# A two-block network on one core: x loaded first, stage ends by token block, two norm sums on GpSimd

## The chip, the core and the metric

The kernel runs on one NeuronCore of a Trainium2 chip, in Bass, with every engine programmed by hand and every dependence written as a semaphore. Below, PE is TensorE (its matmuls), PEld its weight loads, DVE is VectorE, ACT is ScalarE, POOL is GpSimd and SP is SyncE, which issues most DMAs. The metric is the device time of one execution in microseconds (us); less is better.

## The reference, cut to what matters

256 tokens of width 1024 pass through two blocks; all is float32.

```
x   = x + rms_norm(mix(rms_norm(x) @ w_in) @ w_out)          # NSA, pooling and SGU mixers
x   = x + rms_norm(memory_attention(rms_norm(x), mem) @ w_mo) # stage "mo"
x   = x + rms_norm((gelu(conv(h @ w_up)_gate) * conv(h @ w_up)_val) @ w_down),  h = rms_norm(x)  # "up", "down"
h   = concat(16 meta tokens, x)                               # 272 tokens from here
h   = h + (silu(z) * b * conv(c * xin)) @ conv_out_w          # proj = rms_norm(h) @ conv_in_w
h   = h + mlstm(rms_norm(h) @ mlstm_in_w) @ mlstm_out_w       # 4 heads, 8 gate columns
out = rms_norm(h)[16:]
```

`rms_norm(x) = x * rsqrt(mean(x^2) + eps) * gain`. The kernel leaves the factor 1/rms out of an operand and multiplies it into the product, so the sum of squares of a norm is needed only after the first products that use the new x.

## The kernel before, in words

**Weights.** 287 chunks of 128x1024 float32 go through four slots. SP loads chunk n into `raw` (after `lo_ready` of chunk n-4), ACT copies it to `w_hi` (rounded to fp32r, `hi`, after `chunk_done` of chunk n-4), DVE writes the rest, `w_lo = raw - w_hi` (`lo`). PE forms each product in three fp32r matmuls: hi with hi, hi with lo, lo with hi. ACT and DVE run three chunks ahead of PE (`ahead`). Chunks have an order by name in `_LAYOUT`: kc, vc, vsw, ... mo, up, down, conv_in, conv_out, lk, lq, ...

**Opening.** SP issues the gains (first 80 columns of params), chunk 0, both halves of x (k tiles 0 to 3 and 4 to 7), then chunks 1 to 3. ACT makes `XH` (hi of gain times x) for eight k tiles, DVE makes `XL`. PE first runs `keep_warm(WARM_START)`, products of constants that nothing reads, then chunk kc, one k tile at a time, as `normed_lo` grows; then vc and vsw.

**Stage ends of mo and down** (`rows_stage`, u = 0 and 1). These two stages put tokens on the partitions. The output has two column halves and two blocks b of 128 tokens. In the second half each chunk is used for block 0 and then for block 1. ACT squares the finished block (`rows_norm`, L736), takes the root (L739), DVE inverts it and scales (`rows_update`, L1965 to L1969), ACT scales one part of block 1 (L743), PE turns the blocks back (L1297), DVE adds them to the residual XR (L1974), ACT makes XH (L700) and DVE XL (L1910). PE then runs `side_by_side`: the first three chunks of the next stage together, k tile by k tile, as XH (`raw_hi`) and XL (`raw_lo`) come.

**Norm sums.** ACT writes squares of x into `SQ` and counts `sq_ready`. In `stat_x` PE sums all eight k tiles with 64 recorded small matmuls against ones (32 products); in `stat_sum` GpSimd has added k tiles 0 to 6 into `SS` before (`sum_squares`, six additions, each waiting for the last), and PE needs 8 products. Before the change, norms X2 (after mo) and H0 (after down) use `stat_x`, and H1 (after conv_out) uses `stat_sum`. ACT takes the root, DVE inverts it, PE spreads it (`spread_rstd`, L1214), ACT copies it into `rstd`.

**GpSimd's order** around this: sums of the first norm; during up, 44 elementwise operations (L615, L617); then the DMA of the mLSTM gate weights (`lgate_w`), their scaling (L628), four memsets and the mask built by affine selects (L634, L637); then one multiplication in each round of conv_in (L642).

**H1 and the mLSTM gates.** After conv_out PE runs chunk lk 0 whole, then `gate_products` (L1354) and `stat_sum`; the spread stands in the middle of lk 1. DVE can empty the accumulator of lk 0 (L2431) only when `rstd` is there; there are two accumulators, so lk 2 waits for it.

Of the kernel before, what the change touches and what calls it, by code (L numbers as in the profile page):

```python
# [87 lines left out]
WARM_START = 10  # L88
# [50 lines left out]
def build(nc, weights, x_in, mem_in, meta_in, params, final_gain, rel_bias, onehot, lgate_w, out, bias_rows):  # L139
    with ExitStack() as ctx:  # L140
# [193 lines left out]
        def spread_mem():  # L334
# [9 lines left out]
        gate_loaded, gate_scaled, gate_summed, l_gate_summed, gate_parted = (  # L344
            sem("gate_loaded"), sem("gate_scaled"), sem("gate_summed"), sem("l_gate_summed"), sem("gate_parted"))
# [158 lines left out]
        def _(sp):  # L504
# [42 lines left out]
        def _(pool):  # L547
# [63 lines left out]

            def ffn_pool(p, i, hidden, rest):
# [12 lines left out]
            pool.dma_start(lgate_raw, lgate_w).then_inc(gate_loaded, 16)  # L625
            pool.wait_ge(gate_loaded, 16)
# [30 lines left out]
        def _(act):  # L657
# [403 lines left out]
            for m in range(KT):  # L1061
                ahead(CHUNK["lq"] + m)
                if m == 0:
                    act.wait_ge(l_gate_summed, 1)
# [134 lines left out]
        def _(pe):  # L1199
# [68 lines left out]
            def rows_stage(name, u, per, x, ready):  # L1268

                t = TILE[name]  # L1270
                for half in range(2):
                    o = [acc(t + b)[:, :] if half == 0 else SC[:, span(b, 512)] for b in range(2)]
                    for c in range(per):
# [4 lines left out]
                        for b in range(2):  # L1278
# [4 lines left out]
                            if half and b == 0 and c == per - 1:  # L1283
                                last.then_inc(rows_half, 1)
                        last.then_inc(chunk_done, 1)
                keep_warm(WARM, PTB)
                for b in range(2):
                    for k in range(KT):
# [9 lines left out]
                        if b and k % 2:  # L1298
                            last.then_inc(rows_turned, 1)
                keep_warm(WARM_SPREAD)  # L1300
# [48 lines left out]
            def gate_products(raw_w):  # L1349
# [6 lines left out]
                last.then_inc(gate_summed, 1)  # L1356
# [75 lines left out]
            chunk(CHUNK["kc"], TILE["kc"], xh, xl, S, ready=x_ready)  # L1432
# [284 lines left out]
            stat_x(NORM_H0, 3, T)  # L1717
# [8 lines left out]

            for m in range(KT):
                chunk(CHUNK["lk"] + m, TILE["lk"] + m, xha, xla, T, between=(lambda: spread_rstd(NORM_H1, T)) if m == 1 else None,
                      ready=raw_ready(RAW_H1) if m == 0 else None)
                if m == 0:  # L1730
# [1041 lines left out]
```

## Time and profile before

| | |
|---|---|
| median of 3 runs | 923.64 us (923.40 to 923.68) |
| profiled execution, its own time | 922.43 us |
| its span | 920.70 us |
| PE busy | 908.9 us, 99% |
| DVE busy | 655.7 us, 71% |
| ACT busy | 532.2 us, 58% |
| POOL busy | 131.6 us, 14% |
| mean of DMA traffic | 171 GB/s |

How to read it: the span runs from the first to the last recorded instruction; the profiled execution took 1.73 us more than its span and 1.21 us less than the median. A matmul's record is longer than the distance to the next one, since matmuls are pipelined, so PE's busy share hides short gaps: distances between starts tell more.

### The profile page before, as it was taken

The page shows a single profiled execution, that of the slowest core. Times are in us where ns is not written, and L with a number is a line of the kernel's source. Part 1 is how long each engine was busy: PE and PEld are TensorE (multiplying, and loading weights), DVE is VectorE, ACT ScalarE, POOL GpSimd, SP SyncE. Part 2 cuts the span into 40 slices and gives each one's busy share as a digit, 9 for nine tenths or more (in the row PEclk, how much of TensorE's full clock was granted, in tenths as well). Part 3 has the DMA queues.
Part 4 walks back from the last instruction along what each step waited for, and adds up shares of the span by engine and source line. Part 5 has one row for each costly group of instructions (what it writes and reads, how often), then busy time and mean ns, then how long its engine had stood idle before and what let it go on. Part 6 is the DMA issues. An engine that isn't in the chain of part 4 may idle for free.

```text
span 920.7 us, 19094 instructions
## 1 busy us (share of the span) xinstructions
PE 908.9 (99%) x6971; PEld 853.1 (93%) x6971; DVE 655.7 (71%) x1115; ACT 532.2 (58%) x904; POOL 131.6 (14%) x131
## 2 busy tenths in 40 slices
PE   8999999999999999999999999999999999999997
PEld 7998899998999998889999999999999998888886
DVE  4898877545899998447877777766578476767743
ACT  6868586545776765546444444444464567666643
POOL 2211010000056566000111111101010000000000
PEclk9999999999999999999999999999999999999999
DMA  8853434435345555652555555555355444455561
GB/s 303 278 169 109 149 109 166 158 117 184 135 161 204 197 193 207 211 203 96 190 174 179 175 174 178 171 196 180 139 184 185 159 159 135 160 166 161 182 196 56
DMA packets 44995, 157.58 MB, mean 171 GB/s; under 512 B 6067, under 2 KB 7219, under 8 KB 44684
## 3 DMA queue, kind: packets, MB, share of 16 engines
q1 hardware_dynamic: 44380, 155.03, 49.4%
q0 software_dynamic: 560, 1.79, 0.7%
q8 instruction: 38, 0.62, 0.3%
q14 instruction: 17, 0.14, 0.0%
HBM read 155.74 MB, written 1.06 MB: 170 GB/s over the span
## 4 chain that ended last, share of the span: by engine, by line
PE 93%; DVE 3%; ACT 2%; issue 1%; DMA 1%; SPq 0%; DVEq 0%; ACTq 0%
PE acc L1311 13%; PE acc L1313 13%; PE acc L1312 13%; PE scores L1311 6%; PE scores L1313 6%; PE scores L1312 6%; PE acc L1264 4%; PE acc L1266 4%; PE acc L1265 4%; PE scores L1265 2%; PE scores L1266 2%; PE scores L1264 2%; PE outs L1266 2%; PE outs L1264 2%; PE outs L1265 2%; PE acc L1395 1%
## 5 line engine op out<-in xcount | busy, mean ns | idle before, releaser
L1884 DVE TENSOR_TENSOR w_lo<-raw,w_hi 128x1024 fp32r<-128x1024 f32 x287 | 353.4, 1238 | 97.0 <-ACT w_hi L665 96.5
L665 ACT ACTIVATE w_hi<-raw 128x1024 fp32r<-128x1024 f32 x287 | 301.3, 1056 | 150.4 <-PE acc L1313 62.7
L1311 PE MATMUL acc<-XH,w_hi 128*128 128x256 f32 (+1 forms) x616 | 176.2, 286 | 0.5 <-DVE Y L2431 0.3
L1312 PE MATMUL acc<-XL,w_hi 128*128 128x256 f32 (+1 forms) x616 | 173.5, 282 | 0.0
L1313 PE MATMUL acc<-XH,w_lo 128*128 128x256 f32 (+1 forms) x616 | 173.5, 282 | 0.0
L1311 PE MATMUL scores<-XH,w_hi 128*128 128x272 f32 (+1 forms) x424 | 120.1, 283 | 0.0
L1313 PE MATMUL scores<-XH,w_lo 128*128 128x272 f32 (+1 forms) x424 | 119.7, 282 | 0.0
L1312 PE MATMUL scores<-XL,w_hi 128*128 128x272 f32 (+1 forms) x424 | 119.7, 282 | 0.0
L1311 PEld LDWEIGHTS acc<-XH,w_hi 128*128 128x128 f32 x616 | 115.9, 188 | 3.0 <-issue 2.4
L1312 PEld LDWEIGHTS acc<-XL,w_hi 128*128 128x128 f32 x616 | 116.0, 188 | 0.1
L1313 PEld LDWEIGHTS acc<-XH,w_lo 128*128 128x128 f32 x616 | 115.9, 188 | 0.0
L1311 PE MATMUL acc<-AH,w_hi 128*128 128x272 f32 (+1 forms) x360 | 103.9, 289 | 0.0
L1313 PE MATMUL acc<-AH,w_lo 128*128 128x272 f32 (+1 forms) x360 | 102.5, 285 | 0.0
L1312 PE MATMUL acc<-AL,w_hi 128*128 128x272 f32 (+1 forms) x360 | 102.5, 285 | 0.0
L1311 PEld LDWEIGHTS scores<-XH,w_hi 128*128 128x128 f32 x424 | 79.8, 188 | 0.2
L1312 PEld LDWEIGHTS scores<-XL,w_hi 128*128 128x128 f32 x424 | 79.8, 188 | 0.0
L1313 PEld LDWEIGHTS scores<-XH,w_lo 128*128 128x128 f32 x424 | 79.8, 188 | 0.0
L1311 PEld LDWEIGHTS acc<-AH,w_hi 128*128 128x128 f32 x360 | 68.0, 189 | 0.1
L1312 PEld LDWEIGHTS acc<-AL,w_hi 128*128 128x128 f32 x360 | 68.1, 189 | 0.0
L1313 PEld LDWEIGHTS acc<-AH,w_lo 128*128 128x128 f32 x360 | 68.0, 189 | 0.0
L642 POOL TENSOR_TENSOR AR<-AR,rstd 128x272 f32<-128x272 f32 x16 | 26.1, 1634 | 214.2 <-DVE AR L2391 214.2
L615 POOL TENSOR_TENSOR AR<-AR 128x256 f32<-128x256 f32 x22 | 32.4, 1473 | 131.1 <-DVE AR L2348 126.6
(539 smaller groups left out, 1801.7 us busy)
## 6 DMA issues: line engine op xcount, KB each, us to landing
raw<-weights SPq DMA_DIRECT2D x287, 512.0 KB, 3.4
cst<-params SPq DMA_DIRECT2D x1, 1080.5 KB, 10.7
XR<-x_t SPq DMA_DIRECT2D x2, 512.0 KB, 6.1
Y<-mem_t SPq DMA_DIRECT2D x1, 1024.0 KB, 9.6
AR<-bias_rows POOLq DMA_DIRECT2D x4, 256.0 KB, 5.4
out<-AR SPq DMA_DIRECT2D x2, 512.0 KB, 2.6
AR<-final_gain POOLq DMA_DIRECT2D x1, 512.0 KB, 6.1
AR<-lgate_w POOLq DMA_DIRECT2D x1, 192.0 KB, 2.6
```

What stands on the lines that cost most here:

```text
L615: nc.gpsimd.tensor_tensor(Ft[:, p % 2, :], Gt[:, p % 2, :], Vt[:, p % 2, :], ALU.mult).then_inc(act_ready, 1)
L642: nc.gpsimd.tensor_tensor(Yc, Yc, rstd[:, :], ALU.mult).then_inc(c_scaled, 1)
L665: nc.scalar.activation(w_hi[:, n % SLOTS, :], raw[:, n % SLOTS, :], ACT.Copy).then_inc(hi_ready, 1)
L1264: nc.tensor.matmul(o, hi, w_hi[:, w, c], start=first, stop=False)
L1265: nc.tensor.matmul(o, hi, w_lo[:, w, c], start=False, stop=False)
L1266: return nc.tensor.matmul(o, lo, w_hi[:, w, c], start=False, stop=last)
L1311: nc.tensor.matmul(o, wh, h, start=start, stop=False)
L1312: nc.tensor.matmul(o, wh, l, start=False, stop=False)
L1313: return nc.tensor.matmul(o, wl, h, start=False, stop=stop)
L1395: nc.tensor.matmul(o, xh(k)[:, b * P:(b + 1) * P], wh, start=(k == 0), stop=False)
L1884: V.tensor_tensor(w_lo[:, s, :], raw[:, s, :], w_hi[:, s, :].bitcast(F32), ALU.subtract).then_inc(lo_ready, 1)
```

## The change

SP loads the first half of x first, then chunk 0 in two halves of 512 columns, then the second half of x; the gains move to ACT's DMA queue. ACT and DVE split chunk 0 by halves, between the k tiles of x, and PE has a `first_chunk` of its own that waits for the parts one by one. `WARM_START` goes from 10 to 7. In `rows_stage` the last two chunks are both used for block 0 first and then both for block 1; `keep_warm(WARM, PTB)` ahead of the turning is gone. The third chunk of the next stage gets its `w_lo` from GpSimd (`lo_behind`) and no longer from DVE, which signals `lo_ready` for it after waiting for `behind_lo`. DVE adds k tiles 0 and 1 by token block. Norms X2 and H0 use `stat_sum`, with `sum_squares` on GpSimd. `keep_warm(1, PTB)` in front of the loop over up is gone. The gate products and the sum of H1 stand in the middle of lk 0, and the spread in front of lk 1. The DMA of the gate weights now follows `lo_behind("down")` on GpSimd.

```diff
-WARM_START = 10
+WARM_START = 7
@@ sync
-            sp.dma_start(cst[:, 0:GAINS], params[:, 0:GAINS]).then_inc(gains_loaded, 16)
-            load(0)
             load_x(0)
+            sp.dma_start(raw[:, 0, 0:512], weights[0][:, 0:512]).then_inc(first_loaded, 16)
+            sp.dma_start(raw[:, 0, 512:1024], weights[0][:, 512:1024]).then_inc(weights_loaded[0], 16)
             load_x(1)
@@ gpsimd
+            def lo_behind(name, per):
+
+                n = CHUNK[name] + 2 * per - 1 + AHEAD
+                w = n % SLOTS
+                pool.wait_ge(hi_ready, n + 1)
+                nc.gpsimd.tensor_tensor(w_lo[:, w, :], raw[:, w, :], w_hi[:, w, :].bitcast(F32), ALU.subtract).then_inc(behind_lo, 1)
+
+            lo_behind("mo", 4)
+            sum_squares(lambda m: pool.wait_ge(sq_ready, KT * 2 + m + 1), META)
...
-            pool.dma_start(lgate_raw, lgate_w).then_inc(gate_loaded, 16)
-            pool.wait_ge(gate_loaded, 16)
+            lo_behind("down", FFN_TILES // 2)
+            pool.dma_start(lgate_raw, lgate_w).then_inc(row_loaded, 16)
+            pool.wait_ge(row_loaded, 16)
...
+            sum_squares(lambda m: pool.wait_ge(sq_ready, KT * 3 + m + 1), 0)
@@ scalar, rows_norm
-                for c in range(2 * per):
+                for c in range(2 * per - 1):
                     ahead(n + c)
...
                     else:
+                        ahead(n + 2 * per - 1)
                         wait_chunk(act, n + 2 * per - 1)
@@ scalar, opening
+            act.dma_start(cst[:, 0:GAINS], params[:, 0:GAINS]).then_inc(gains_loaded, 16)
...
-            hi(0)
             act.wait_ge(gains_loaded, 16)
             for k in range(KT):
+                if k == 2:
+                    act.wait_ge(first_loaded, 16)
+                    nc.scalar.activation(w_hi[:, 0, 0:512], raw[:, 0, 0:512], ACT.Copy).then_inc(first_parts, 1)
+                if k == KT // 2:
+                    act.wait_ge(weights_loaded[0], 16)
+                    nc.scalar.activation(w_hi[:, 0, 512:1024], raw[:, 0, 512:1024], ACT.Copy).then_inc(hi_ready, 1)
@@ tensor, rows_stage
-                    for c in range(per):
+                    for c in range(per if half == 0 else per - 2):
...
-                keep_warm(WARM, PTB)
+                for b in range(2):
+                    for c in (per - 2, per - 1):
+                        n = CHUNK[name] + per + c
+                        if b == 0:
+                            pe.wait_ge(lo_ready, n + 1)
+                        for j in (2 * c, 2 * c + 1):
+                            last = rows_product(n, o[b], x, j, b, j == 2 * per - 1)
+                        if b:
+                            last.then_inc(chunk_done, 1)
+                    if b == 0:
+                        last.then_inc(rows_half, 1)
@@ tensor
-            stat_x(NORM_X2, 2, S)
+            stat_sum(NORM_X2, 2, lambda: pe.wait_ge(sq_ready, 3 * KT), S)
             ffn_pe(0, 3, lambda: spread_rstd(NORM_X2, S))
-            keep_warm(1, PTB)
...
-            stat_x(NORM_H0, 3, T)
+            stat_sum(NORM_H0, 3, lambda: pe.wait_ge(sq_ready, 4 * KT), T)
...
+            def gates_and_sums():
+
+                for k in (KT - 2, KT - 1):
+                    wait_evacuated(pe, TILE["conv_out"] + k)
+                gate_products(lgate_raw)
+                stat_sum(NORM_H1, 4, lambda: pe.wait_ge(sq_ready, SQ_H1 + KT), T)
+
             for m in range(KT):
-                chunk(CHUNK["lk"] + m, TILE["lk"] + m, xha, xla, T, between=(lambda: spread_rstd(NORM_H1, T)) if m == 1 else None,
+                if m == 1:
+                    spread_rstd(NORM_H1, T)
+                chunk(CHUNK["lk"] + m, TILE["lk"] + m, xha, xla, T, between=gates_and_sums if m == 0 else None,
@@ vector, rows_update
+                    if b:
+                        dve.wait_ge(first_turned, u + 1)
+                        for k in (0, 1):
+                            add_block(k, 0)
...
-                add(0)
-                add(1)
+                dve.wait_ge(rows_turned, 4 * u + 1)
+                for k in (0, 1):
+                    add_block(k, 1).then_inc(x_updated, 1)
+                dve.wait_ge(behind_lo, u + 1)
+                V.memset(small[:, 159:160], 0.0).then_inc(lo_ready, 1)
```

**Where instructions stand.** GpSimd, from the last operations of stage up to the loop over conv_in; before (w_lo, raw and SQ are named in the text above, AR and cst hold many small tensors, `SS` is a part of cst):

```order
L617 TENSOR_TENSOR ML<-AR,MH 128x256 [waits act_hi]
L625 DMA AR<-lgate_w 128x384
L628 TENSOR_TENSOR AR<-AR,cst 128x256 [waits gate_loaded]
...
L634 AFFINE_SELECT AR<-AR 32x32 [waits pool_steps]
L637 AFFINE_SELECT AR<-AR 32x16 [waits pool_steps]
L640 UNCONDITIONAL_BRANCH [waits pool_steps]
```

The same stretch of the changed kernel:

```order
L629 TENSOR_TENSOR ML<-AR,MH 128x256 [waits act_hi]
L619 TENSOR_TENSOR w_lo<-raw,w_hi 128x1024 [waits hi_ready]
L638 DMA AR<-lgate_w 128x384
L641 TENSOR_TENSOR AR<-AR,cst 128x256 [waits row_loaded]
...
L650 AFFINE_SELECT AR<-AR 32x16 [waits pool_steps]
L557 TENSOR_TENSOR cst<-SQ 128x272 [waits sq_ready,pool_steps]
L557 TENSOR_TENSOR cst<-cst,SQ 128x272 [waits sq_ready,pool_steps] x5
```

The DMA and all that follows it now stand behind a subtraction that waits for a late chunk, and six additions stand behind the mask.

ACT in the opening, before:

```order
L673 ACTIVATE small<-small 128x1 [waits consts_ready]
L665 ACTIVATE w_hi<-raw 128x1024 [waits weights_loaded0]
L758 ACTIVATE XH<-XR,cst 128x256 [waits x_loaded0,gains_loaded]
L758 ACTIVATE XH<-XR,cst 128x256 x3
L758 ACTIVATE XH<-XR,cst 128x256 [waits x_loaded1]
```

And in the changed kernel:

```order
L765 DMA cst<-params 128x80
L687 ACT_TABLE_LOAD
L687 ACTIVATE small<-small 128x1 [waits consts_ready]
L779 ACTIVATE XH<-XR,cst 128x256 [waits x_loaded0,gains_loaded]
L779 ACTIVATE XH<-XR,cst 128x256
L773 ACTIVATE w_hi<-raw 128x512 [waits first_loaded]
L779 ACTIVATE XH<-XR,cst 128x256 x2
L776 ACTIVATE w_hi<-raw 128x512 [waits weights_loaded0]
L779 ACTIVATE XH<-XR,cst 128x256 [waits x_loaded1]
```

The first two k tiles of x now come ahead of the weights, whose copy is split.

DVE at the end of mo, from the first inverted root to the first XL, before:

```order
L1968 TENSOR_SCALAR Y<-acc,small 128x512 [waits rows_rstd]
L1969 TENSOR_SCALAR Y<-scores,small 128x512
L1965 RECIPROCAL small<-small 128x1 [waits rows_root]
L1969 TENSOR_SCALAR Y<-scores,small 128x512 [waits rows_rstd]
L1974 SCALAR_TENSOR_TENSOR XR<-turned,cst,XR 128x256 [waits rows_turned]
```

And in the changed kernel:

```order
L2032 TENSOR_SCALAR Y<-acc,small 128x512 [waits rows_rstd]
L2033 TENSOR_SCALAR Y<-scores,small 128x512
L2019 SCALAR_TENSOR_TENSOR XR<-turned,cst,XR 128x128 [waits first_turned]
L2029 RECIPROCAL small<-small 128x1 [waits rows_root]
L2033 TENSOR_SCALAR Y<-scores,small 128x512 [waits rows_rstd]
L2019 SCALAR_TENSOR_TENSOR XR<-turned,cst,XR 128x128 [waits rows_turned]
L2045 MEMSET small 128x1 [waits behind_lo]
```

The additions of k tiles 0 and 1 are halved, block 0's stand ahead of block 1's root, and the memset that releases the chunk waits for GpSimd.

## Rows read from the trace of the kernel before

**Rows 1.** The page, part 4: the chain that ended last, by engine.

```profile
PE 93%; DVE 3%; ACT 2%; issue 1%; DMA 1%; SPq 0%; DVEq 0%; ACTq 0%
```

**Rows 2.** Timeline, opening: start us, length us, engine, line, operation, tiles, count, idle before.

```profile
1.74 0.98 SPq L512 DMA_DIRECT2D XR<-x_t  x2
...
4.02 4.49 PE L1257 MATMUL scores<-ident,ones_d 128*128 128x128 f32 x20 [4.02 <-POOL sel L577]
...
7.50 3.31 ACT L758 ACTIVATE XH<-XR,cst 128x256 fp32r<-128x256 f32 x8 [1.71 <-DMA XR<-x_t]
8.11 3.26 DVE L1990 SCALAR_TENSOR_TENSOR XL<-XR,cst,XH 128x256 fp32r<-128x256 f32 x8 [1.07 <-ACT XH L758]
...
12.92 1.06 ACT L665 ACTIVATE w_hi<-raw 128x1024 fp32r<-128x1024 f32 x1 [0.21 <-DMA raw<-weights]
```

**Rows 3.** The two loads of x (line L512), issue to landing.

```profile
DMA to landing us min/median/max: 5.7/6.1/6.6
```

**Rows 4.** Timeline of PE, end of mo.

```profile
228.79 0.61 PE L1257 MATMUL turned<-ident,ones_d 128*128 128x128 f32 x4
229.67 0.66 PE L1297 MATMUL turned<-ident,Y 128*128 128x128 f32 x4 [0.28 <-DVE Y L1968]
...
230.91 0.80 PE L1297 MATMUL turned<-ident,Y 128*128 128x128 f32 x4
...
231.98 0.61 PE L1257 MATMUL scores<-ident,ones_d 128*128 128x128 f32 x4
232.56 0.36 PE L1325 MATMUL acc<-XH,w_hi 128*128 128x256 f32 x1
```

**Rows 5.** Timeline of ACT, ends of mo and down.

```profile
227.62 0.60 ACT L736 ACTIVATE SQ<-scores 128x512 f32<-128x512 f32 x1 [0.24 <-PE scores L1266]
...
228.99 0.60 ACT L736 ACTIVATE SQ<-scores 128x512 f32<-128x512 f32 x1 [0.35 <-PE scores L1266]
...
230.38 0.84 ACT L743 ACTIVATE Y<-acc,small 128x256 f32<-128x256 f32 x2 [0.38 <-DVE small L1965]
...
237.63 0.62 ACT L701 ACTIVATE SQ<-XR 128x512 f32<-128x512 f32 x1
...
412.19 1.06 ACT L665 ACTIVATE w_hi<-raw 128x1024 fp32r<-128x1024 f32 x1 [1.66 <-PE scores L1266]
```

**Rows 6.** Timeline of PE, the sums of norm H0 and of norm H1.

```profile
427.55 1.16 PE L1204 MATMUL outs<-SQ,ones_d 128*32 128x68 f32 x64
...
662.00 0.30 PE L1204 MATMUL outs<-SQ,ones_d 128*32 128x68 f32 x8
```

**Rows 7.** Timeline of POOL, from the gate weights' DMA to the mask's last select.

```profile
360.95 0.59 POOL L625 DMA_DIRECT2D AR<-lgate_w  x1
363.61 1.54 POOL L628 TENSOR_TENSOR AR<-AR,cst 128x256 f32<-128x256 f32 x1 [2.07 <-DMA AR<-lgate_w]
...
366.90 0.19 POOL L637 TENSOR_SCALAR_AFFINE_SELECT AR<-AR 32x16 f32<-32x16 f32 x1
...
368.41 0.19 POOL L637 TENSOR_SCALAR_AFFINE_SELECT AR<-AR 32x16 f32<-32x16 f32 x1
```

**Rows 8.** Timelines of POOL and DVE, two-input operations alone and side by side.

```profile
64.74 6.58 POOL L606 TENSOR_TENSOR ML<-Y,MH 128x256 fp32r<-128x256 f32 x8 [20.36 <-ACT MH L887]
...
443.47 1.69 POOL L642 TENSOR_TENSOR AR<-AR,rstd 128x272 f32<-128x272 f32 x1 [5.77 <-DVE AR L2391]
...
653.63 0.77 POOL L555 TENSOR_TENSOR cst<-cst,SQ 128x272 f32<-128x272 f32 x1 [5.15 <-ACT SQ L1054]
653.66 1.04 DVE L1910 SCALAR_TENSOR_TENSOR XL<-XR,cst,XH 128x272 fp32r<-128x272 f32 x1
```

**Rows 9.** Timeline of PE, lk 1 and the first product of lk 2.

```profile
663.83 1.00 PE L1214 MATMUL outs<-root,pick 128*128 128x68 f32 x8
...
666.08 0.29 PE L1313 MATMUL acc<-XH,w_lo 128*128 128x272 f32 x1
666.64 0.36 PE L1311 MATMUL acc<-XH,w_hi 128*128 128x272 f32 x1 [0.28 <-DVE Y L2431]
```

More of the change, by code:

```diff
@@ L343, in build @@
         rel_loaded = sem("rel_loaded")
-        gate_loaded, gate_scaled, gate_summed, l_gate_summed, gate_parted = (
-            sem("gate_loaded"), sem("gate_scaled"), sem("gate_summed"), sem("l_gate_summed"), sem("gate_parted"))
+        first_turned, behind_lo = sem("first_turned"), sem("behind_lo")
+        first_loaded, first_parts = sem("first_loaded"), sem("first_parts")
+        gate_scaled, gate_step = (
+            sem("gate_scaled"), sem("gate_step"))
         token_rstd, shifted, rf_ready, rf_hi, gate_exp, swapped = (
@@ L1299, in rows_stage @@
                             last.then_inc(rows_turned, 1)
+                        elif k == 1:
+                            last.then_inc(first_turned, 1)
                 keep_warm(WARM_SPREAD)
@@ L1355, in gate_products, with first_chunk @@
                                                 start=(first == 0), stop=(first > 0))
-                last.then_inc(gate_summed, 1)
+                last.then_inc(gate_step, 1)
+            def first_chunk(n, t):
+                s, o = n % SLOTS, acc(t)[:, 0:S]
+                pe.wait_ge(first_parts, 1)
+                for k in range(2):
+                    x_ready(k)
+                    nc.tensor.matmul(o, w_hi[:, s, k * P:(k + 1) * P], xh(k), start=(k == 0), stop=False)
+                    nc.tensor.matmul(o, w_hi[:, s, k * P:(k + 1) * P], xl(k), start=False, stop=False)
+                pe.wait_ge(first_parts, 2)
+                for k in range(2):
+                    nc.tensor.matmul(o, w_lo[:, s, k * P:(k + 1) * P], xh(k), start=False, stop=False)
+                for k in range(2, KT):
+                    if k == KT // 2:
+                        pe.wait_ge(lo_ready, n + 1)
+                    x_ready(k)
+                    last = three(o, n, k, xh(k), xl(k), False, k == KT - 1)
+                last.then_inc(chunk_done, 1)
             def high_first(n, t):
@@ L1430, in spread_x @@
                 spread_rstd(NORM_X, S)
-            chunk(CHUNK["kc"], TILE["kc"], xh, xl, S, ready=x_ready)
+            first_chunk(CHUNK["kc"], TILE["kc"])
             high_first(CHUNK["vc"], TILE["vc"])
@@ L1951, in rows_ahead @@
             def rows_ahead(name, u, per):
-                for c in range(2 * per):
+                for c in range(2 * per - 1):
                     ahead(CHUNK[name] + c)
@@ L1961, in rows_update, with add_block @@
                 t = TILE[name]
+                def add_block(k, b):
+                    cols = slice(META + b * P, META + (b + 1) * P)
+                    return V.scalar_tensor_tensor(out=XR[:, k, cols], in0=turned_rows(k)[:, span(b, P)], scalar=col(post, k),
+                                                  in1=XR[:, k, cols], op0=ALU.mult, op1=ALU.add)
                 for b in range(2):
                     rstd_b = row_rstd[:, b:b + 1]
+                    if b:
+                        dve.wait_ge(first_turned, u + 1)
+                        for k in (0, 1):
+                            add_block(k, 0)
                     dve.wait_ge(rows_root, 2 * u + b + 1)
@@ L1985, in _ @@
             V.memset(small[:, 158:159], EPS).then_inc(consts_ready, 1)
-            lo(0)
             dve.wait_ge(gains_loaded, 16)
             for k in range(KT):
+                if k == 2:
+                    dve.wait_ge(first_parts, 1)
+                    V.tensor_tensor(w_lo[:, 0, 0:512], raw[:, 0, 0:512], w_hi[:, 0, 0:512].bitcast(F32), ALU.subtract).then_inc(first_parts, 1)
+                if k == KT // 2:
+                    dve.wait_ge(hi_ready, 1)
+                    V.tensor_tensor(w_lo[:, 0, 512:1024], raw[:, 0, 512:1024], w_hi[:, 0, 512:1024].bitcast(F32), ALU.subtract).then_inc(lo_ready, 1)
                 dve.wait_ge(normed_hi, k + 1)
```

17 lines of the change are left out of this document (6 added, 11 removed).

## The prediction, on record before the changed kernel was run

> **What bounds the kernel now.** I read the page's chain first, since it says who sets the end: PE holds 93% of it and DVE and ACT together 5% [rows 1]. So a part of the change is worth what it takes from PE's sequence or from a gap in it. Next I read PE's timeline at the four places that the diff touches, for gaps between starts. At the end of mo PE runs two idle products (four records of 0.11 us), then waits for DVE's first scaled block, turns, waits once more at 230.91, and begins the next stage at 232.56 [rows 4]. The 64 records of a norm's sum take 1.16 us where the short form takes 0.30 for its last half [rows 6]. In lk, PE stands 0.44 us (666.08 to 666.64 from start to start, 0.12 of it the matmul) in front of lk 2 until DVE has emptied lk 0 [rows 9]. The opening waits for x [rows 2]. Last I read GpSimd, which the change loads with new work that PE waits for [rows 7, 8].
>
> **The opening.** Before, the first half of x lands 5.7 us after its issue at 1.74, thus at 7.4; ACT makes XH from 7.50 on, one k tile each 0.41 us (3.31 / 8), so k tile 4 at 9.15. The second half, issued 0.5 later, lands 6.6 us after, at 8.8 [rows 2, 3]. In the changed kernel as many bytes still stand ahead of the second half (the first half and chunk 0), so it lands at 8.8 again, within a few tenths. k tiles 0 to 3 are ready long before and PE finishes them early, but k tile 4 starts at 8.8 in place of 9.15: the gain is what lies between, 0.35, not the 2 us by which x begins earlier. Upper end: XL ends at 11.37, the last three products and vc's 24 at 0.114 each bring PE to 14.4, where vsw wants chunk 3's hi, which ACT, held by the load, has at 12.92 + 1.06 = 13.98 [rows 2]; that leaves 0.5. Lower end 0. The three warm products saved are hidden: PE would only wait for x. I take **-0.4**.
>
> **Ends of mo and down.** Twelve products of a chunk take 1.06 + 1.66 = 2.72 us, 0.227 each [rows 5]. Block 0 is now finished 12 instead of 6 products before the end, 1.36 us earlier; from ACT's square at 227.62 to the turning at 229.67 took 2.05 [rows 4, 5], so block 0 is ready at about 228.3 and the turning starts at 228.8, 0.87 earlier. But block 1 is finished when it was: its square starts at 228.99, ACT's scale at 230.38, and the turning of block 1 begins at 230.91 as before and ends at 231.98 [rows 4, 5]. The 0.87 us becomes a wait between the blocks. Behind it two idle products remain, 0.45 us, and the side-by-side products can begin at 232.45 in place of 232.56, if XH is there; halved additions let DVE be 0.2 earlier, so it is. Each end gives **-0.1** (0 to -0.3). ACT's copy of the third chunk is held until 1.36 us before the end (the chunk that frees its slot now ends there) and lies in ACT's idle time. GpSimd's subtraction of 1024 columns is in no row: eight of 256 took 6.58 us, of which one DVE subtraction of 1.22 held them up, so (6.58 - 1.22) / 2 = 2.7; by the slope from one of 272 (0.77) it is 2.4 at least [rows 8]. It starts when ACT's copy is done, about at the last product, and DVE wants it 2.9 us later: hidden, by 0.2 to 0.5. If DVE's two-input operations held it for 1.2, all that DVE queues behind `behind_lo` (every further addition to XR, hence XH and PE) would be 0.9 late, at both ends.
>
> **Sums by GpSimd.** 64 records at 1.16 us become 16; H1's 8 took 0.30 with its tail, and from starts of records the saving is 0.8 a norm, **-1.6** for two, if the sum is there [rows 6].
>
> For X2: the last squares end at 237.63 + 0.62 = 238.25; one addition takes 0.77 alone, and PE wants the sum 2.6 us after that (240.9; H0's analogue is 427.55 against squares that end 3.2 before) [rows 5, 6, 8]. What speaks against it is sharing: 0.77 became 1.69 where a DVE subtraction of two SBUF tensors had begun first, and DVE's L1910 took 1.04 for 0.5 where GpSimd had begun first, so whoever is second waits for the first [rows 8]. [...] Six additions push DVE back by up to 0.7 each while it makes XL, whose slack I read as 0.2 to 1.9 us along the eight k tiles, and chunk 3's w_lo, a subtraction of 1.2 us right behind XL, comes 1 to 2 us later. I take 0.3 of stall, 0 to 0.9. X2: **-0.5**.
>
> For H0 the same six additions stand behind more. In the changed order GpSimd does, from the end of down: subtraction (414.75 to 417.1; the copy of ACT that was at 412.19 comes 1.36 later), DMA, scaling, memsets and mask, which took 368.60 - 360.95 = 7.65 us before [rows 5, 7], thus to 424.75, then six additions at 0.77 + 0.07 between linked instructions = 5.05, to 429.8. PE wants the sum at 427.45. **The stall is 2.35 us**, less 0.8 saved: **+1.5**. Nothing covers it: the squares are long done and PE's next product stands behind. Lower end: the 7.65 holds 0.8 of scaling under a DVE subtraction and 1 or so of held selects (one without, from 366.90 on, costs 0.27); with 5.6, the sum is there at 427.7 and the stall 0.3, so H0 gains 0.5. Upper end: one more DVE subtraction in the way, 1.2, and 0.3 for the slow price of 1024 columns: 431.3, a stall of 3.9, H0 at +3.0.
>
> **The idle product of the loop** costs 0.11 us at most; the loop over conv_in is entered without one and its gap is as long, so I take 0.
>
> **lk.** Gates and sum move 1.6 us forward, PE's own work stays. The spread comes at 662.1 instead of 663.83, before which ACT's table load and root and DVE's inversion just fit; `rstd` is 1.6 us earlier and lk 2's wait is gone: **-0.45** (0 to -0.5) [rows 9].
>
> **Sum.** -0.4 - 0.2 - 0.5 + 1.5 - 0.45 = -0.05, say -0.1, against the profiled execution's own 922.43 us (span 920.70): 922.3. The median of the runs is 1.2 above it, so 923.5.
>
> **Rivals.**
> (a) *Sums in time.* GpSimd's path at H0 runs unhindered and ends at 427.7 or earlier: all other gains stand, the mask costs nothing. -0.5 - 0.2 - 0.8 - 0.6 - 0.5 = -2.6, 921.0. For it: DVE leaves idle gaps in this stretch; against: even unhindered work ends behind PE's wish by my rows. It needs less than 5.3 us from DMA to mask. 0.16.
> (b) *The sum of H0 late by more than 4 us*, the other side: in 0.5 us slices beside XL and the w_lo behind it each of the nine small operations waits for a DVE operation (0.5 each is 2 us more than in the rows). From a stall of 4.2 us on the kernel is slower by 0.2%: 2.35 + 2 = 4.35 gives +2.0, 925.6. 0.08.
> (c) *PE's clock.* [...] The changed kernel has three new idle stretches: 1.3 us between k tiles 3 and 4 of the opening, 1.2 us between the two blocks, 2.4 us at H0. If one makes PE fall back, products at half rate for some 4 us (as long as the opening ran so) lose 2 us: 925.5. No row before shows a stretch this long inside the run. [...] 0.09.
> (d) *The block order wins more.* Block 1's wait is shorter than I read: at most 0.4 more at each end, 922.7. Within the forecast's range.
> The forecast, a stall of 0.5 to 4 us at H0 with the small gains paid back, has 0.67.
>
> **How the numbers follow.** 0.2% of 923.64 is 1.85 us, about what a measurement of this kernel can tell from no change. The forecast with (d) spans 921.9 to 925.1 and is nearly all within 921.8 and 925.5; (a) falls below, (b) and (c) above. Faster: 0.16 and 0.02 of the forecast, 0.18. Slower: 0.08 + 0.06 (half of (c) and more) + 0.01, 0.15. Same: 0.67. The range 921.3 to 925.4 leaves out the lower half of (a) and most of (b) and (c), under 0.2.
>
> **What would show it.** After: x's second half lands at 8.8 and PE's kc ends 0.3 to 0.5 earlier; PE idles 1.2 us between the blocks; the sums are 16 records; the stretch in front of H0's sum shows PE waiting for POOL 2 to 3 us, with the mask's selects at 421 to 425; in front of lk 2 no wait. The prediction is wrong if POOL's last addition for H0 ends before 427.6, if XL is so late that PE waits inside the side-by-side products, or if records of PE double in length behind a gap.

## The result, and the profile after

The changed kernel takes **927.61 us** (median of ten executions, 925.98 to 929.30) against 923.78 for the kernel before, run beside it (ten executions too, one of them apart at 3517 us): 1.0041 times as long, 95% interval 1.0031 to 1.0051. Comparisons leave disturbed executions out. It is slower by 3.8 us; the profiled execution took 927.97 (span 926.2), 5.54 more than the profiled one of before. The longest waits of PE in the changed kernel:

```profile
engine line waited for: us in total, times, longest us
PE scores L1278 <- POOL sel L579: 4.0, 1, 4.0
PE outs L1225 <- POOL cst L557: 2.2, 1, 2.2
PE turned L1326 <- ACT Y L758: 1.9, 2, 0.9
```

The 2.2 us at the H0 sum and the two 0.9 us between the token blocks are new. They don't add up to 5.54 us, so the table cuts both traces at the same products (from start to start, us; the stretches that it leaves out agree within 0.01):

| stretch | before | after | difference |
|---|---|---|---|
| start to the first product of mo | 206.81 | 206.76 | -0.05 |
| last product of mo to the first of side by side, up | 4.00 | 3.72 | -0.28 |
| side by side, first to last | 8.14 | 8.44 | +0.30 |
| from there to the first product of down (X2 sum, up loop) | 114.10 | 117.45 | **+3.35** |
| last product of down to the first of side by side, conv_in | 4.07 | 3.80 | -0.27 |
| last of side by side to the last stage's first rows product (H0 sum, conv, lk) | 335.55 | 338.05 | **+2.50** |

**The opening**, timeline of PE (start us, length us):

```profile
7.07 0.58 PE L1395 MATMUL acc<-XH,w_hi 128*128 128x256 f32 x1
7.44 0.42 PE L1396 MATMUL acc<-XL,w_hi 128*128 128x256 f32 x1
...
9.58 0.41 PE L1344 MATMUL acc<-XH,w_lo 128*128 128x256 f32 x1
9.80 0.32 PE L1342 MATMUL acc<-XH,w_hi 128*128 128x256 f32 x1
9.96 0.28 PE L1343 MATMUL acc<-XL,w_hi 128*128 128x256 f32 x1
```

PE's first product comes at 7.07 instead of 8.74, but up to 9.80 the products follow at 0.21 us from start to start, then at 0.118. At vc's low part PE is 0.66 us ahead, and still at 122 us.

**End of mo**, PE; it answers to [rows 4]:

```profile
228.74 0.60 PE L1326 MATMUL turned<-ident,Y 128*128 128x128 f32 x4
...
230.71 0.80 PE L1326 MATMUL turned<-ident,Y 128*128 128x128 f32 x4 [0.93 <-ACT Y L758]
...
232.22 0.35 PE L1356 MATMUL acc<-XH,w_hi 128*128 128x256 f32 x1
```

Block 0 is turned at once, block 1 at 230.71, and the next stage starts at 232.22.

**The H0 sum**, GpSimd and PE; they answer to [rows 6, 7]:

```profile
418.00 2.35 POOL L619 TENSOR_TENSOR w_lo<-raw,w_hi 128x1024 fp32r<-128x1024 f32 x1 [53.68 <-ACT w_hi L679]
420.30 0.59 POOL L638 DMA_DIRECT2D AR<-lgate_w  x1
423.10 0.91 POOL L641 TENSOR_TENSOR AR<-AR,cst 128x256 f32<-128x256 f32 x1 [2.21 <-DMA AR<-lgate_w]
...
426.02 0.47 POOL L650 TENSOR_SCALAR_AFFINE_SELECT AR<-AR 32x16 f32<-32x16 f32 x1
426.57 1.06 POOL L557 TENSOR_TENSOR cst<-SQ 128x272 f32<-128x272 f32 x1
427.71 5.05 POOL L557 TENSOR_TENSOR cst<-cst,SQ 128x272 f32<-128x272 f32 x5
```

```profile
430.13 0.41 PE L1362 MATMUL acc<-XL,w_hi 128*128 128x272 f32 x2
...
432.82 0.33 PE L1225 MATMUL outs<-cst,ones_d 128*32 128x68 f32 x8 [2.16 <-POOL cst L557]
432.97 0.33 PE L1225 MATMUL outs<-SQ,ones_d 128*32 128x68 f32 x8
433.23 0.60 PE L1342 MATMUL scores<-XH,w_hi 128*128 128x272 f32 x1
433.62 0.43 PE L1343 MATMUL scores<-XL,w_hi 128*128 128x272 f32 x1
...
436.11 0.65 PE L1235 MATMUL outs<-root,pick 128*128 128x68 f32 x3
```

GpSimd ends at 432.76 what PE wanted at 430.6. PE stands idle for that time; I call this the stand, 2.45 us from start to start. Behind it the records of the products are 0.43 us long where they were 0.29, and they start every 0.23 us instead of every 0.12: half rate. The windows view (busy us of PE, PEld, DVE, ACT, POOL, then the granted clock as a share of full speed) shows the clock:

```profile
430.00:434.00 4.00, 1.84 (x25) 1.50 (x24) 0.31 (x1) 1.71 (x3) 2.53 (x4) 0.89 0.40 131
434.00:438.00 4.00, 4.00 (x26) 4.00 (x25) 1.57 (x3) 2.19 (x4) 0.00 (x0) 0.69 0.35 127
438.00:442.00 4.00, 4.00 (x32) 3.83 (x32) 3.78 (x8) 2.20 (x3) 0.00 (x0) 1.00 0.13 30
```

Between 433.1 and 436.5 the share is 0.50 throughout; before and behind it is 1.00.

**The up loop.** No wait is listed there, the clock is 1.00, and yet a round of 96 products takes 11.31 us instead of 10.88. Groups of PE in 300 to 310 us, kernel before, then changed (count, busy us, mean ns of one):

```profile
L1311 PE MATMUL acc<-XH,w_hi 128*128 128x256 f32 x16 | 4.4, 276 | 0.0
```

```profile
L1342 PE MATMUL acc<-XH,w_hi 128*128 128x256 f32 x16 | 4.5, 281 | 0.0
```

276 ns goes with 113.3 ns from start to start, 281 ns with 117.8 (called 113 and 118 below). The 4.5 ns are in every product. The slow pace is not confined to the changed code: both kernels show both paces in other stages. In the changed trace the loop begins at the fast one, up to here:

```profile
256.02 0.28 PE L1343 MATMUL scores<-XL,w_hi 128*128 128x256 f32 x1
256.13 0.28 PE L1344 MATMUL scores<-XH,w_lo 128*128 128x256 f32 x1
256.24 0.38 PE L1342 MATMUL acc<-XH,w_hi 128*128 128x256 f32 x1
256.46 0.28 PE L1343 MATMUL acc<-XL,w_hi 128*128 128x256 f32 x1
256.58 0.28 PE L1344 MATMUL acc<-XH,w_lo 128*128 128x256 f32 x1
```

```profile
254.89 1.22 DVE L1938 TENSOR_TENSOR w_lo<-raw,w_hi 128x1024 fp32r<-128x1024 f32 x1
```

DVE ends the new chunk's `w_lo` at 256.11. The record of the chunk's first product, at 256.24, is 0.10 us longer than the others and the next one starts 0.1 us late: a short wait, most likely for that `w_lo`. From 256.46 to 358.0 all products are at 118 ns. That stretch is 863 products x 4.45 ns = 3.8 us. With 0.1 for the wait, less 0.67 for the shorter X2 sum, it gives 3.3 of the 3.35 us. The idle product that is gone won nothing here: the loop's first product stands 0.25 us behind the last one ahead of it, 0.26 in the kernel before, since its weight load now waits 0.17 us, at 245.24, for DVE to empty the accumulator.

### The profile page after: what moved, and what is told of

It is laid out like the page before. It is cut to its first block, busy times and chain, and to the rows that moved or that the text cites. A ratio compares the mean times of both kernels' runs of the same rounds, so it can differ in the third digit from the quotient of the medians.

```text
span 926.2 us, 18905 instructions
## 1 busy us (share of the span) xinstructions
PE 911.5 (98%) x6859; PEld 856.8 (93%) x6859; DVE 655.7 (71%) x1120; ACT 531.8 (57%) x905; POOL 143.3 (15%) x145
## 3 DMA queue, kind: packets, MB, share of 16 engines
q0 software_dynamic: 560, 1.79, 0.7%
HBM read 155.74 MB, written 1.06 MB: 169 GB/s over the span
## 4 chain that ended last, share of the span: by engine, by line
PE 93%; DVE 2%; ACT 2%; POOL 1%; issue 1%; DMA 0%; POOLq 0%; DVEq 0%; ACTq 0%
PE acc L1342 13%; PE acc L1343 13%; PE acc L1344 13%; PE scores L1342 6%; PE scores L1344 6%; PE scores L1343 6%; PE acc L1287 4%; PE acc L1286 4%; PE acc L1285 4%; PE scores L1287 2%; PE scores L1286 2%; PE scores L1285 2%; PE outs L1286 2%; PE outs L1287 2%; PE outs L1285 2%; PE acc L1444 1%
## 5 line engine op out<-in xcount | busy, mean ns | idle before, releaser
L1287 PE MATMUL acc<-w_hi,AL 128*128 128x512 f32 x128 | 50.0, 390 | 0.0
## 6 DMA issues: line engine op xcount, KB each, us to landing
AR<-bias_rows POOLq DMA_DIRECT2D x4, 256.0 KB, 6.0
raw<-weights SPq DMA_DIRECT2D x2, 256.0 KB, 4.9
```

Source lines behind the costliest of these rows:

```text
L1287: return nc.tensor.matmul(o, lo, w_hi[:, w, c], start=False, stop=last)
```

## The experiments

Eighteen runs. "Loop stretch" is the row of the table from the end of side by side to down, "H0 stretch" its last row. Both are read from the one profiled execution of a run; the medians are of all its executions, and a ratio compares them with those of the kernel before, run beside them. The letters (A, B, C, ...) name the theories of the expectations. "Draw" and "odds" mean that executions of one kernel come out at one pace or the other.

**1. The idle product back, the mask first, both, and the kernel before without its idle product.**

```
keep_idle:       ffn_pe(0, 3, ...)
               + keep_warm(1, PTB)            # ahead of the up loop
mask_first:    - lo_behind("down", ...)       # ahead of the gate DMA on GpSimd
               + lo_behind("down", ...)       # behind the mask's selects, ahead of sum_squares
before_no_idle: - keep_warm(1, PTB)           # in the kernel before
```

> The changed kernel with the one idle product put back in front of the up loop. In the trace of the changed kernel the first product of the loop's second chunk waits 0.1 us at 256.24 for a w_lo that VectorE ends at 256.11, and from there to 358 all products of 256 columns follow at 118 ns instead of 113 ns (a round of 96 takes 11.31 us instead of 10.88). Theory A (such a short wait sets the pace of what follows): the product gives the low half 0.1 us more, no wait, rounds of 10.88, about 923.4 us (927.6 - 4.3 + 0.1). Rival B (the pace is drawn anew at each execution, whatever stands in front of the loop): 926 to 929 us, as the changed kernel. Rival C (pace comes from where the code lies, not from the wait): either pace, but the wait at 256 may be there with 113 ns behind it.

> The changed kernel with GpSimd's low half of the third chunk of down moved behind its gate load, scaling and mask (whose 7.65 us then lie inside the rows products of down, as in the kernel before). Theory D (GpSimd's late sum costs twice: TensorE stands 2.45 us at 430.4, and its granted clock is 0.69 over 434 to 438 behind it): 3.8 us less, 923.8 us, no wait at the H0 sum and a clock of 1.00 over 430 to 442. Rival E (only the stand counts, as the prediction had it): 2.2 to 2.4 us less, 925.3 us. The up loop is expected at 11.31 us a round still.

> Both edits together. Theories A and D: 927.6 - 4.2 - 3.8 = 919.6 us, 4 us under the kernel before. With B instead of A: 923.8. With E instead of D: 921.1.

> The kernel before without its one idle product in front of the up loop, nothing else. Theory A: the low half is still 0.2 to 0.3 us ahead of the product that reads it (256.49 against 256.8), so no wait, rounds of 10.88, 923.6 us. Rival F (the idle product itself, or a loop entered without a pause, sets the pace): rounds of 11.31, 928 us.

| | median us | ratio, 95% | loop stretch | H0 stretch |
|---|---|---|---|---|
| keep_idle | 928.23 | 1.0049 (1.0036 to 1.0063) | 117.76 | 338.11 |
| mask_first | 920.57 | 0.9966 (0.9953 to 0.9978) | 117.46 | 334.32 |
| both_back | 924.38 | 1.0005 (0.9996 to 1.0014) | 117.46 | 334.32 |
| before_no_idle | 927.38 | 1.0037 (1.0024 to 1.0051) | 118.10 | 335.59 |

The H0 part is clean: the sum in time takes 3.73 us off that stretch (D, not E), and the clock stays up:

```profile
430.00:434.00 4.00, 4.00 (x47) 3.75 (x46) 1.88 (x4) 3.62 (x6) 0.00 (x0) 1.00 0.41 131
434.00:438.00 4.00, 4.00 (x33) 3.82 (x32) 3.78 (x8) 2.31 (x3) 0.00 (x0) 1.00 0.51 146
```

The up loop refutes A as the only way to the slow pace: keep_idle has no wait at 256 and runs at 118 ns from 245.4 on, and both_back, with the product, has the wait. Taking the product out of the kernel before costs 4 us in all five executions, putting it into the changed one wins nothing: its absence (F) is enough by itself, but not the only cause. And the profiled execution of mask_first, at 924.07, was its slowest of six; the others reached down to 919.49.

**2. Parts alone, and idle products.** Each idle product stands in the trace as two records; each one behind the first took 0.21 us in mf_idle4, not the 0.11 that I expected of it.

```
opening_only: the kernel before + first_chunk, order of loads, WARM_START 7
sums_only:    the kernel before + both sum_squares on GpSimd, stat_sum in place of stat_x
mf_idle4:     mask_first + keep_warm(4, PTB) ahead of the up loop
mf_round:     mask_first + keep_warm(1, PTB) at the end of each round
```

> The kernel before with the change's opening alone (loads with x first, the first key chunk in two halves, seven idle products instead of ten). In the changed kernel's trace this part is 0.66 us ahead up to 122 us, and 0.15 from 142 on because the products between 123 and 142 follow at 118 instead of 113 ns. Theory A2 (the pace of a long stretch is drawn where the stretch starts, by timing, and is kept to its end): -0.15 to -0.7 us where the up loop keeps 10.88 us a round, and about +3.7 us where it is drawn at 11.31; nothing in between. Theory G (the opening is worth 0.4 as predicted and touches nothing else): 923.0 us.

> The kernel before with GpSimd adding the squares of X2 and H0 (its gate load and mask lie ahead of it inside down, no low half on GpSimd), the idle product kept. The two sums are in time: -0.7 each from the trace (16 products instead of 64, 1.03 to 0.36 us). Theory G: 922.4 us. Theory A2: 922.4 or, with the up loop at 11.31 us a round, 926.7.

> The version with the mask first (920.6 us, executions from 919.5 to 924.1; its profiled one ran at 113 ns from 245.5 to 256.0, waited 0.1 us for w_lo there and ran at 118 ns to 357.8) with four idle products in front of the up loop, 0.45 us, so that the low half of the loop's second chunk is 0.35 us early. Theory A (the short wait makes the pace slow): no wait, 113 ns, all executions within 0.5 us of 920.0. Theory A2 (drawn where the stretch starts, by timing): the loop's first products decide; all near 920 or all near 924, the profile shows one pace from 245 to 358. Theory B (drawn anew in each execution): both values among the runs.

> The version with the mask first and one idle product of 128 columns at the end of every round of the up loop (10 rounds, 0.11 us each, 1.1 us). Theory A2: every such product is a new draw, so that the rounds of one execution have either pace, and the time lies 1.1 us over a mixture: 921 to 925 us with both paces in the trace. Rival C (the pace belongs to the code of the loop): one pace in all rounds.

opening_only: 922.40 (ratio 0.9984, 0.9975 to 0.9993), loop stretch 114.07, at 113 ns. sums_only: 926.16 (1.0031, 1.0019 to 1.0043), loop stretch 117.45, the slow case of A2; its H0 stretch is 334.85, 0.70 under that of before. mf_idle4: 921.04 (0.9969, 0.9957 to 0.9980), with six executions from 920.55 to 921.87 and the profiled one at 925.18, at 118 ns from 246.1 on with no wait (both values among the runs, as B has it). mf_round: 925.14 (1.0019, 1.0011 to 1.0028); in one execution both paces stand side by side, groups in 258 to 266 and 268 to 278 us:

```profile
L1342 PE MATMUL acc<-XH,w_hi 128*128 128x256 f32 x11 | 3.0, 276 | 0.0
```

```profile
L1342 PE MATMUL acc<-XH,w_hi 128*128 128x256 f32 x15 | 4.2, 281 | 0.0
```

Rounds 2, 5 and 8 of its trace ran at 113 ns, the others at 118. So the same instructions in the same loop take either pace (against C), and what stands between two stretches of products can change it.

**3. Does a short wait set it?** mask_first once more for a second profile; the late low half made early; and the reverse, a wait put into the kernel before.

```
lo_early, after_lo_early (in mask_first, in the changed kernel):
+ if third and v: ahead(n, i)        # ahead of ffn_taps instead of behind
before_lo_late:
+ if third and v: ...; V.tensor_tensor(SS[:, 0:256], raw[...], w_hi[...], ALU.subtract)   # cut: its wait for hi_ready
```

> The version with the mask first once more, unchanged, for a second profile: its executions lay at 919.5 to 920.7 (four), 922.8 and 924.1, and the profiled one was that of 924.1, with the up loop at 113 ns to 256.0 and 118 ns to 357.8. Theory A2 (two paces, drawn per execution): if this profiled execution takes about 920, its products follow at 113 ns up to 354; if about 924, at 118 from 256 on. Rival H (every profiled execution of this kernel is slow there, and the others differ elsewhere): 924 again, or 920 with 118 ns in the loop.

> The version with the mask first, and VectorE's low half of the loop's second chunk (254.9 to 256.1 there, read by TensorE at 256.1) put ahead of the two tap sums, so that it ends near 255.4. Theory A3 (a stretch keeps its pace until a wait of about 0.1 us, behind which it is 118 ns): no wait at 256, 113 ns from 245.5 to the end of the loop, every execution between 919.4 and 920.8. Rival B (the pace is drawn in each execution, waits or not): executions at 920 and at 924 as before.

> The changed kernel with that one low half early, all else as changed. A3: the up loop at 10.88 us a round, 4.1 us less: 927.6 - 4.1 = 923.5 us, the H0 stand of 2.45 us and its clock still there. Rival B: 926 to 929 as before, or both.

> The kernel before with one more VectorE operation of 256 columns (about 0.42 us, into a buffer that nobody reads) ahead of the low half of the loop's second chunk (255.27 to 256.49, read by TensorE at 256.8), which makes it end at about 256.9: a wait of 0.1 to 0.2 us. A3: the wait costs 0.15 by itself, and the products behind it follow at 118 ns for ten rounds: 923.4 + 4.3 = 927.7 us. Rivals C and B: 923.5 us.

| | median us (ratio, 95%) | executions, us | profiled one: us, loop |
|---|---|---|---|
| mask_first_2 | 919.99 (0.9974, 0.9956 to 0.9993) | eight at 919.5 to 920.3; 923.9, 924.4, 927.3 | 924.44, 118 ns from 245.4 |
| lo_early | 924.12 (1.0003, 0.9991 to 1.0016) | 920.2, 921.0, 921.2, 921.8; seven at 924.0 to 925.1 | 921.78, 113 ns throughout |
| after_lo_early | 928.01 (1.0048, 1.0034 to 1.0062) | 926.8 to 928.3 | 928.03, 118 ns from 260 |
| before_lo_late | 927.37 (1.0049, 1.0034 to 1.0064) | 923.41; 927.1 to 929.6 | 923.41, 113 ns throughout |

The edits changed the wait otherwise than meant. In lo_early PE stood 0.5 us for the `w_lo` of the next chunk, at 260.35, and in before_lo_late for the chunk meant, at 257.75, but for 0.5 us instead of 0.1 to 0.2:

```profile
257.02 0.28 PE L1313 MATMUL scores<-XH,w_lo 128*128 128x256 f32 x1
257.75 0.38 PE L1311 MATMUL acc<-XH,w_hi 128*128 128x256 f32 x1 [0.46 <-DVE w_lo L1884]
257.97 0.28 PE L1312 MATMUL acc<-XL,w_hi 128*128 128x256 f32 x1
```

Both went on at 113 ns behind it, after_lo_early, with the same wait of 0.5 us, at 118. So a wait of that size doesn't force the slow pace. The short wait of A3 was not tested by these edits, and the traces of all runs don't clear it: the six that have the 0.1 us (changed kernel, changed_again, both_back, sums_only, mask_first, mask_first_3) all enter the loop at 113 ns and are at 118 behind it, of the five with a wait of 0.4 to 0.5 us three stay at 113 and two go to 118, and the two that enter at 113 and have none stay there. The four other executions of before_lo_late lie 3.7 to 6.2 us over its profiled one, and the median of the kernel before beside them is 922.88: one inserted operation changed how often the loop is fast. Against rival H speaks the profiled 921.78 of lo_early, though it is not the same kernel; all three profiled executions of mask_first were slow, and that profiling shifts its odds is not excluded.

**4. The last open points.** The changed kernel again, mask_first a third time, idle products over the H0 stand, the stage ends alone.

```
warm_h0:   + keep_warm(20, PTB)      # ahead of stat_sum(NORM_H0, ...)
ends_only: the kernel before + rows_stage, rows_norm, rows_update and lo_behind of the changed one
```

> The changed kernel once more, unchanged, for a second profile and more executions. Its first ten lay from 926.0 to 929.3. From the traces so far: 924.2 with the up loop slow and the H0 sum in time; with the H0 stand of 2.3 us 926.5; with the clock's fall behind it 928 to 929. Theory A2 with J (the changed kernel nearly always draws the slow pace in the up loop, and the clock falls in most executions): 926 to 929 us, loop rounds of 11.31 us; an execution with the loop fast would be 922 to 924.5, and few or none come. Rival K (the changed kernel draws as the version with the mask first does, three in four fast, and something else costs the rest): 922 to 925 for most.

> The version with the mask first a third time, for a profile of an execution near 920 us. A2: 113 ns from 246 to the end of the up loop there, about 4.2 us less between the last product of the side-by-side part and the first of down (113.3 to 113.8 us instead of 117.46 and 117.76). If the profiled execution is near 924 again, 118 ns.

> The changed kernel with 20 idle products of 128 columns (2.2 us) between the side-by-side part and the H0 sum, where TensorE stands 2.45 us. Theory D (stand and clock both cost): the stand is filled, the clock stays at 1.00 over 430 to 442, and 1.5 to 1.8 us come back: from the last side-by-side product to the output's first product 336.5 instead of 338.05 us. Rival L (what follows the stand is slow for another reason, the late sum's chain on VectorE and ScalarE): 338.0 still, at a granted clock of 1.00.

> The kernel before with the two stage ends by token block alone (GpSimd's low halves and the 0.85-us later mask with them). From the traces: the end of mo 3.72 instead of 4.00 us and the end of down 3.80 instead of 4.07, so -0.55 us where the paces are those of the kernel before: 922.6 us. With the up loop slow: 926.9. The prediction had -0.2.

changed_again: 927.87 (1.0038, 1.0025 to 1.0051; executions 926.18 to 928.80), loop stretch 117.45, H0 stretch 337.85: J, not K, though on this chip mask_first had no execution near 920 either. mask_first_3, on the same chip, the third for this kernel: 924.93 (1.0013, 1.0004 to 1.0022), none of eleven under 923.6, the profiled one at 118 ns from 256.0 on, loop stretch 117.44. The same kernel is 0.3% faster than the kernel before on two chips and 0.1% slower on a third. ends_only: 928.02 (1.0047, 1.0033 to 1.0062), ten executions from 927.38 to 931.77 and one at 923.59. The profiled one (928.15) has 3.72 us at the end of mo and 3.80 at the end of down as the changed kernel has, then PE waits 0.4 for a `w_lo` at 258.9, and the loop runs at 118 ns.

warm_h0, windows as above:

```profile
430.00:434.00 4.00, 4.00 (x37) 4.00 (x36) 0.00 (x0) 1.06 (x1) 2.84 (x4) 1.00 0.42 131
434.00:438.00 4.00, 4.00 (x48) 3.78 (x47) 1.66 (x2) 2.14 (x3) 0.00 (x0) 1.00 0.00 0
```

The 20 products took 4.55 us, twice what was planned, so they overfilled the stand: the sum began 4.68 us behind the last side-by-side product instead of 2.45, 2.23 later, and the kernel as a whole took 928.98 us (1.0056, 1.0042 to 1.0070), more than the changed one. But the H0 stretch grew only from 338.05 to 338.77: 1.5 came back, 1.3 in the twelve products ahead of the spread (1.58 us instead of 2.88) and 0.2 in the spread. This is the clock's share, by itself (D, not L). In mask_first the sum begins 0.22 us behind the last side-by-side product, so of its 3.73 us 2.45 - 0.22 = 2.23 are the stand, and 1.50 are left for the clock: the same by another way.

**5. What decides the pace?**

```
x2_old:       mask_first, but stat_x(NORM_X2, 2, S), keep_warm(1, PTB) as in the kernel before
x2_old_idle4: the same with keep_warm(4, PTB)
```

> The version with the mask first, with the X2 sum and the idle product in front of the up loop as in the kernel before (64 products, one idle product; each idle product stands in the trace as two records and takes 0.22 us, not 0.11). Rows it keeps: opening, stage ends, H0 sum on GpSimd, gates in lk. Theory M (the way the X2 stage enters the loop decides the odds: the kernel before and the one with the opening alone enter at 113 ns and stay, every one with another X2 stage was profiled slow): 113 ns, 920.3 us. Rival N (the low half that GpSimd makes at the end of mo leaves VectorE late, a wait at 256 to 260 as in the kernel with the ends alone, and a draw behind it that is mostly slow): 924.5 us.

> The same with four idle products instead of one, 0.67 us more, so that no low half is late in the loop's first round. M: 113 ns, 921.0 us. N: no wait, the pace of the loop's entry is kept: 921.0 if the entry is as that of the kernel before, 925.2 if four idle products enter at 118 ns as in the version with four of them tried before.

x2_old: twelve executions, of which one at 998.9 stands apart; five at 921.2 to 922.6 and six at 924.6 to 926.8, median 924.74 (1.0009, 0.9996 to 1.0022). The profiled one, 922.59, ran at 113 ns behind a wait of 0.5 us for `w_lo`. x2_old_idle4: 925.28 (1.0030, 1.0018 to 1.0042), none under 925.1, the profiled one 118 ns from 246.2 on with no wait. M is refuted. N had the wait right but not what follows it as a rule; what is left is a draw whose odds each edit changes.

## Why the prediction was wrong

The forecast was 923.5 us, within 0.2% of before; it came out 927.61.

**The step that failed is the cost of nothing for the entry of the up loop.** "The idle product of the loop costs 0.11 us at most; ... so I take 0", and in the X2 sum and the stage end I priced only stalls. I worked with one price per product in the loop. The traces hold two: the 863 slow products of the changed trace cost 3.8 us, all 960 would cost 4.3, more than any of my terms. As to the idle product's own time, 0 was right for this trace. Of the twenty profiled executions (with the two given), five have the up loop at 113 ns throughout (loop stretch 114.1 to 114.8), fourteen at 118 from 260 us at the latest (117.4 to 119.0), mf_round both. The executions of the kernel before gather at 923 (95 of 111 under 924.3) and its profiled one is fast; all of the changed kernel's sixteen are at 925.98 or above, and both profiled ones are slow. Single kernels have executions in two groups 3 to 4 us apart, with the profiled ones falling where their pace says (lo_early 921.78 and before_lo_late 923.41 at 113 ns, mask_first_2 924.44 at 118), so I take it that the pace makes the groups. That is an inference: no kernel has one profiled execution at each pace, and other stretches vary too: from the start to mo the twenty traces take 206.2 to 208.2 us.

That the change brought the slow pace is shown by its parts, each put alone into the kernel before, by the times of all executions: the opening leaves the loop fast (eleven of eleven), while the X2 and H0 sums on GpSimd (seven of seven), the stage ends (ten of eleven) and the idle product left out (five of five) each make it slow.

**Rival (c), the clock, came true** where I had given it 0.09, at the H0 stand: 1.5 us, not 2. The 2 us came from the opening, where the 20 records of the kernel before follow every 0.22 us [rows 2], with the windows view at 1.00 there too, and the four at 228.79 every 0.11 [rows 4]. I had held stand and clock apart as two cases, though in these runs the one brings the other; with the stand of 2.35 us forecast, the clock's price belonged in that term. The granted clock was 1.00 before the stand, 0.69 behind it, and 1.00 with it filled, and all four profiled executions with a stand here (2.0 to 2.45 us) have the fall, to 0.57 to 0.69 over 434 to 438. Between the token blocks, at the ends of mo and of down (1.2 us from start to start), it stayed at 1.00. The idle stretch that I named in the opening did not come: ScalarE turned to the second half of x at 8.29 already, not at 8.8, and PE ran at half rate from its first product until 9.80 and so never stood for it. The half rate ate most of the 1.7 us by which it began earlier.

By terms, from the traces:

| term | predicted | measured |
|---|---|---|
| opening | -0.4 | -0.66 up to 122 us; -0.05 at mo: 0.51 given back at 118 ns between 123 and 142, 0.1 behind. This is a draw too: over all traces mo begins at 206.88 on average with the new opening (fifteen) and at 207.46 with the old (five), -0.58 |
| ends of mo and down | -0.2 | -0.28 and -0.27 |
| X2 sum, idle product | -0.5 | -0.67 and 0, +0.1 of wait; then +3.8 of pace, and +0.30 in side by side |
| H0 sum | +1.5 | -0.70 (sums_only) + 2.23 + 1.50 = +3.0 |
| lk | -0.45 | -0.53 (334.32 against 334.85) |

The H0 stand was predicted at 2.35 and for the right reason; inside it two errors cancel: from DMA to the last select 6.2 us where I had 7.65, and the six additions 6.2 where I had 5.05, since two of them met VectorE's work. That the sum came out near was in part luck. The 0.3 of stall inside the X2 term was my estimate from [rows 8], and the changed trace shows none: beside GpSimd's additions VectorE's last three XL operations took 2.21 us instead of 1.41 and the `w_lo` behind them 1.75 instead of 1.22, and PE's products up to the sum still followed every 0.12 us. GpSimd's subtraction of 1024 columns, bounded at 2.4 to 2.7, took 2.35. The block order went as written, block 1 arriving 0.2 earlier than I read. In lk no wait stands in front of lk 2.

At equal paces the change comes to -0.66 - 0.55 - 0.57 + 3.03 - 0.53 = +0.7 us, where the forecast was -0.1. Of the profiled 5.54 us the other 4.8 are the pace in the main: 3.8 in the loop, 0.3 in side by side, and 0.6 in the opening's gain given back. With the mask ahead of the low half, a one-line move, the change is worth 0.7 - 3.7 = -3.0 us at equal paces; 920.57 and 919.99 were measured against 923.42 and 922.88, and on a third chip, where all executions lay at 923.7 or above, the win was gone.

**What stays open** is what picks the pace. A stretch keeps it over hundreds of products; it changes where something other than the steady sequence comes between (a sum, a spread, an idle product, a wait of 0.1 us), not always, and in either direction. The entries at 245 to 247 us alone gave both for the same code (mask_first: 113 ns in two profiled executions, 118 in one). Odds differ between kernels and, for mask_first, between the three chips that it ran on. I tried waits, the idle products and the X2 stage; none decides alone. The strongest lead left is the wait of 0.1 us, with 118 ns behind it in six traces of six; no run put that wait in, or took it out, by itself. Whether the phase between weight loads and products is the mechanism was only argued: at 118 ns the record of every third weight load is 192 ns long and the others 188, at 113 ns all are 188, which may be an effect.

## What to carry to other kernels

When PE holds nearly all of the chain (93% here), compare the mean time of one matmul, shape by shape and stage by stage, before explaining anything by waits; a difference of 5 ns in 276 was here worth more than all new waits together, and no list of waits shows it. Read the executions one by one: two groups 4 us apart mean that a median tells of odds, and a single profile tells of one draw. And price a stand of PE such as this one together with the half-rate products behind it (here 2.2 + 1.5 us), and look for what queues ahead of the late work on its engine: the gate load and the mask needed only to come first.

## What the runs showed that was not expected

- Products of 128x256 in fp32r, weights of 128 columns, have two steady paces at a granted clock of 1.00: 113.3 and 117.8 ns (276 and 281 ns each in the records), with 1 ns of scatter. The products of 272 columns kept to 123.3 or 123.4 ns in the conv loop of all twenty traces, but side by side, ahead of it, they took 124.5 ns on average in eighteen and 127.7 in two (before_no_idle and changed_again).
- A stand of 2.45 us made the granted clock fall to 0.69 over 434 to 438 us; one of 2.0 us (after_lo_early) made it fall too, to 0.57, and with two of 1.2 us it stayed at 1.00.
- One idle product of 128 columns of plain float32 is two records and 0.21 to 0.23 us (20 took 4.55).
- GpSimd's six additions of 128x272 took 1.06, 0.85, 1.63, 0.76, 0.75 and 0.75 us ([rows 8] have 0.77 alone). The two longest stood beside VectorE's work: the one of 1.63 us began within a 1024-column subtraction of VectorE's, which itself took 1.79 us instead of the usual 1.22.
